# Low parts of the weights by an accumulating transfer onto a negated copy, in a two-layer hybrid trunk kernel

## The chip, the cores and the metric

One core of one Trainium2 chip runs the whole program. The metric is the device time of one execution in microseconds (us). Engines are named as in the profile: PE (TensorE matmul), PEld (its weight load), DVE (VectorE), ACT (ScalarE), POOL (GpSimd), SP (SyncE); ACTq, SPq and POOLq are their instruction queues.

## The reference, cut to what matters

A two-layer decoder trunk of width 1024 runs over 1024 prompt tokens and 32 sample tokens. Per layer: RMSNorm, one input projection to 3592 columns, four token mixers side by side (S5, HGRN2, mLSTM, retention), a gate, one output projection, the residual.

```python
for l in range(DEPTH):                                  # DEPTH = 2
    h = rmsnorm(x, norm_w[l])
    proj = jnp.einsum('bld,de->ble', h, w_in[l])        # (., 1024) x (1024, 3592)
    ...                                                 # four mixers on slices of proj, head norms, gates
    x = x + jnp.einsum('ble,ed->bld', mixed, w_out[l])  # (., 1024) x (1024, 1024)
y = rmsnorm(x, final_norm_w)
```

## The kernel before, in words

**Passes and blocks.** Each layer is done in two passes of 512 prompt tokens; the second pass of a layer (passes 1 and 3) carries the 32 sample tokens too. In a pass the input projection runs over 14 blocks of 256 columns (one, `ml_ifg`, has 264), each block with all 1024 rows of the weights as 8 tiles of 128 rows (`KT` = 8). That makes 56 input blocks (4 x 14). In the text they are numbered from 0 in the order in which they run. The output projection has blocks of its own (`"wo"`), which are used without being split.

**High and low parts.** An input block is multiplied as three products, x high by w high, x high by w low and x low by w high, of tensors of type float32r. `split_high` (ACT, lines 1225 to 1233) rounds the raw weights `wraw` to `whi` in one instruction over 2048 (or 2112) columns. `split_low` (POOL, lines 1179 to 1190) then writes `wlo = wraw - whi` in eight instructions, one for each row tile. `wraw`, `whi` and `wlo` each have two slots. The sample tokens of blocks with tokens on the output's rows (`tiled`, line 2376) are multiplied with `wraw` in plain float32, ahead of the block's other pieces.

**Order.** `make_plan` writes one order of steps, which all engines follow; `PLACES` puts the projection's pieces between the steps of the mixers, so that PE has projection work while DVE and ACT work on a mixer. The split of a block is a step at the first piece of the block before it (`split_after`). There ACT splits, and then asks for the weights of the block after the next (`load_until`, line 1250), which go into the slot of the block that has just begun; for that it waits until this block is split. A split waits for the last piece of the block two back (same slot) and for its own weights.

**What PE waits for.** In the first piece of a block PE waits for each row tile's low part before the three products of that tile (lines 2371, 2372); the order of products is tile by tile. A piece is 24 matmuls: 8 row tiles by three products.

**What else POOL does.** In the plan's order, on the same queue as `split_low`: the powers for the RMSNorm of the token tiles (`power`, lines 1192 to 1200) and for the head norms (lines 1211 and 1214), for which DVE waits.

Of the kernel before, what the change touches and what calls it, by code (L numbers as in the profile page):

```python
# [18 lines left out]
F32 = mybir.dt.float32  # L19
# [6 lines left out]
P = 128  # L26
# [372 lines left out]
def trunk_kernel(nc, inp, out, parts=("hg", "ml", "rt", "s5")):  # L399
    plan = make_plan(parts)  # L400
    ctx = ExitStack()
    with ctx:
# [119 lines left out]
        wraw = sb("wraw", [P, 2, KT, WC])  # L522
        with nc.sbuf_tensor("tail_w", [P, 2, KT, WC], F32) as tail_w:
            pass
        whi = sb("whi", [P, 2, KT, WC], F32R)
        wlo = sb("wlo", [P, 2, KT, WC], F32R)
# [171 lines left out]
        def tail_weights(b):  # L698
            if b < 2:
                return wraw[:, wslot[(LAST, "wo", b)], :, 0:256]  # L700
            return tail_w[:, hslot[(LAST, ("s5_x", "s5_g")[b - 2])], :, 0:256]
# [28 lines left out]
        wlo_done = signal("wlo_done", [b + (g,) for b in in_blocks for g in range(KT)])  # L730
# [160 lines left out]
        def _(sp):  # L891
# [52 lines left out]
            for k in w_loads[:2]:  # L944
                src, width = weight_columns(k)
                sp.dma_start(wraw[:, wslot[k], :, 0:width], src.rearrange("(k p) c -> p k c", p=P)).then_inc(*wr_in[wslot[k]].inc(k))
# [224 lines left out]
        def _(pool):  # L1171
# [49 lines left out]
        def _(act):  # L1221
# [15 lines left out]
            def load_until(i):  # L1237
                while loads and len(w_loads) - len(loads) <= i:
# [11 lines left out]
                    nc.scalar.dma_start(wraw[:, wslot[k], :, 0:width], src.rearrange("(k p) c -> p k c", p=P)).then_inc(*wr_in[wslot[k]].inc(k))  # L1250
# [1086 lines left out]
        def _(pe):  # L2337
# [6 lines left out]
            for s, part in plan:  # L2344
# [12 lines left out]
                elif s[0] == "proj" and part[0] in ("mm", "mm2"):  # L2357
# [3 lines left out]
                    for k in [part[1]]:  # L2361
# [8 lines left out]
                        for kt in range(*((0, 4) if part[0] == "mm" else (4, KT)) if long_piece(k) else (KT,)):  # L2370
                            if k == pieces_of_block(*b)[0]:
                                pe.wait_ge(*wlo_done.at(b + (kt,)))
                            if tiled(k):
                                width = BLOCK[b[1]][2] // 4
                                for g in range(4):
                                    mm = nc.tensor.matmul(bank.t[TS * g:TS * g + TS, 0:width], mixT[:, kt, HALF:W], wraw[:, wslot[b], kt, g * width:(g + 1) * width],
                                                          start=kt == 0, stop=kt == KT - 1)
                                continue
                            for x, w in ((hhi, whi), (hhi, wlo), (hlo, whi)):
                                first, last = kt == 0 and w is whi and x is hhi, kt == KT - 1 and x is hlo  # L2380
                                if BLOCK[b[1]][3] == "ch":
                                    _, c0, ln = piece_psum(k)
                                    c = slice(c0, c0 + ln)
                                    mm = nc.tensor.matmul(bank.t[:, 0:c.stop - c.start], w[:, sl, kt, k[2] * P:(k[2] + 1) * P], x[:, kt, c],  # L2384
                                                          start=first, stop=last)
                                else:
                                    c = slice(k[2] * P, k[2] * P + P)
                                    width = BLOCK[b[1]][2]
                                    mm = nc.tensor.matmul(bank.t[:, 0:width], x[:, kt, c], w[:, sl, kt, 0:width], start=first, stop=last)  # L2389
                        if kt == KT - 1:  # L2390
# [307 lines left out]
                elif s[0] == "out":  # L2698
# [13 lines left out]
                    for kt, row in enumerate(mix_order(n)):  # L2712
                        if r == TS:
                            for g in range(4):
                                mm = nc.tensor.matmul(bank.t[TS * g:TS * g + TS, 0:64], mixT[:, row, k[2] * P:k[2] * P + r], wraw[:, wslot[b], kt, 64 * g:64 * g + 64],
                                                      start=kt == 0, stop=kt == 7)
                            continue
                        mm = nc.tensor.matmul(bank.t[0:r, 0:256], mixT[:, row, k[2] * P:k[2] * P + r], wraw[:, wslot[b], kt, 0:256],  # L2718
# [28 lines left out]
```

## Time and profile before

| What | Value |
|---|---|
| median of 3 runs | 1543.24 us (1541.05 to 1543.25) |
| profiled execution | 1546.32 us, of which the span from its first to its last instruction is 1544.5 us |
| PE busy | 1376.2 us (89% of the span) |
| PEld busy | 1205.4 us (78%) |
| DVE busy | 889.5 us (58%) |
| ACT busy | 549.8 us (36%) |
| POOL busy | 445.5 us (29%) |
| granted TensorE clock, mean | 0.934 |
| DMA | 149.84 MB, 97 GB/s |

An engine's busy share is an average over stages with different limits. A busy PE is not PE at its peak, as matmuls overlap. The chain of work that ended last is followed back from the last instruction, at each step to what released it, or to the instruction before it on its engine; what stands on this chain set the end of this execution.

### The profile page before, as it was taken

How to read it: one execution, taken by the hardware profiler on the slowest of the kernel's cores; microseconds unless marked ns; L12 is line 12 of the kernel's file. 1: busy time of each engine (PE TensorE's matmuls, PEld its weight loads, DVE VectorE, ACT ScalarE, POOL GpSimd, SP SyncE). 2: the span in 40 equal slices, each digit the busy share in tenths (PEclk: the TensorE clock that was granted, in tenths of full speed). 3: DMA queues.
4: the chain of work that ended last, by engine and by line, in shares of the span. 5: the costliest groups of instructions: out<-in, count | busy, mean ns of one | idle time of the engine just before them, and what ended most of it. 6: DMA issues, size and time to landing. Idle time of an engine off the chain costs nothing.

```text
span 1544.5 us, 31690 instructions
## 1 busy us (share of the span) xinstructions
PE 1376.2 (89%) x12391; PEld 1205.4 (78%) x12391; DVE 889.5 (58%) x2670; ACT 549.8 (36%) x1197; POOL 445.5 (29%) x628
## 2 busy tenths in 40 slices
PE   2868899989898999998999899998999999889896
PEld 2757789778786889876787789987878898779665
DVE  4986746463697535555746543656456444644537
ACT  4435443324333533322452334332642533421011
POOL 4341533522002351432310154352200433331001
PEclk9988999989898999998999999997999999999889
DMA  6322123422233423342322333342313415354501
GB/s 176 96 82 71 55 85 110 130 73 87 59 101 120 130 70 108 102 106 70 113 67 86 113 102 112 109 144 59 114 59 118 111 58 125 137 112 95 148 10 59
DMA packets 167563, 149.84 MB, mean 97 GB/s; under 512 B 63440, under 2 KB 155352, under 8 KB 165752
## 3 DMA queue, kind: packets, MB, share of 16 engines
q1 hardware_dynamic: 96696, 76.38, 17.7%
q10 hardware_dynamic: 70720, 71.44, 15.2%
q8 instruction: 100, 1.64, 0.5%
q14 instruction: 47, 0.39, 0.1%
HBM read 124.42 MB, written 23.37 MB: 96 GB/s over the span
## 4 chain that ended last, share of the span: by engine, by line
PE 64%; DVE 19%; ACT 6%; issue 5%; POOL 3%; DMA 1%; SPq 1%; DVEq 0%; ACTq 0%; POOLq 0%
PE psum L2389 17%; PE psum L2384 16%; PE psum L2718 6%; DVE r L1723 4%; PE psum L2696 3%; PE psum L2637 3%; DVE r L2097 3%; PE psum L2548 2%; PE psum L2636 2%; PE psum L2456 2%; POOL rs L1214 1%; ACT r L1504 1%; POOL wlo L1189 1%; PE psum L2634 1%; DVE QE L2118 1%
## 5 line engine op out<-in xcount | busy, mean ns | idle before, releaser
L1189 POOL TENSOR_TENSOR wlo<-wraw,whi 128x256 fp32r<-128x256 f32 (+1 forms) x448 | 345.9, 807 | 425.9 <-ACT whi L1233 425.9
L2389 PE MATMUL psum<-whi,hhi 128*128 128x256 f32 (+1 forms) x896 | 267.7, 299 | 4.3 <-ACT th L1320 2.0
L2389 PE MATMUL psum<-whi,hlo 128*128 128x256 f32 (+1 forms) x896 | 259.0, 289 | 0.0
L2389 PE MATMUL psum<-wlo,hhi 128*128 128x256 f32 (+1 forms) x896 | 258.6, 289 | 0.0
L2384 PE MATMUL psum<-hhi,whi 128*128 128x288 f32 (+2 forms) x672 | 231.7, 345 | 7.8 <-ACT r L1354 5.6
L2384 PE MATMUL psum<-hhi,wlo 128*128 128x288 f32 (+2 forms) x672 | 220.3, 328 | 0.0
L2384 PE MATMUL psum<-hlo,whi 128*128 128x288 f32 (+2 forms) x672 | 220.3, 328 | 0.0
L2718 PE MATMUL psum<-wraw,mixT 128*128 128x256 f32 x768 | 179.8, 395 | 6.8 <-DVE xo L2314 6.8
L2389 PEld LDWEIGHTS psum<-whi,hhi 128*128 128x128 f32 x896 | 176.9, 197 | 11.1 <-issue 7.0
L2389 PEld LDWEIGHTS psum<-wlo,hhi 128*128 128x128 f32 x896 | 177.0, 198 | 0.7 <-issue 0.5
L1211 POOL TENSOR_SCALAR rs<-mv 128x4 f32<-128x4 f32 (+1 forms) x54 | 10.4, 192 | 575.1 <-DVE mv L2280 574.3
L2389 PEld LDWEIGHTS psum<-whi,hlo 128*128 128x128 f32 x896 | 176.1, 196 | 0.0
L2718 PEld LDWEIGHTS psum<-wraw,mixT 128*128 128x128 f32 x768 | 150.2, 198 | 29.8 <-DVE xo L2314 7.8
L2384 PEld LDWEIGHTS psum<-hhi,whi 128*128 128x128 f32 x672 | 129.7, 193 | 23.3 <-issue 12.4
L1233 ACT ACTIVATE whi<-wraw 128x2048 fp32r<-128x2048 f32 (+1 forms) x56 | 107.3, 1916 | 113.1 <-PE psum L2384 54.2
L2384 PEld LDWEIGHTS psum<-hhi,wlo 128*128 128x128 f32 x672 | 129.7, 193 | 12.4 <-issue 3.4
L2384 PEld LDWEIGHTS psum<-hlo,whi 128*128 128x128 f32 x672 | 129.2, 192 | 10.3
L2277 DVE BATCH_NORM_STATS2 stats<-psum 128x6 f32<-128x64 f32 (+1 forms) x144 | 22.3, 217 | 99.0 <-PE psum L2637 98.9
L2637 PE MATMUL psum<-r,ST 128*128 128x64 f32 (+1 forms) x384 | 70.0, 286 | 2.2 <-issue 2.2
L2097 DVE TENSOR_TENSOR r<-r 128x256 f32<-128x256 f32 (+1 forms) x134 | 53.0, 467 | 15.5 <-PE psum L2548 15.4
L2637 PEld LDWEIGHTS psum<-r,ST 128*128 128x128 f32 x384 | 58.4, 203 | 4.0 <-issue 3.7
L1214 POOL TENSOR_TENSOR rs<-rs,epow 128x4 f32<-128x4 f32 (+1 forms) x54 | 56.7, 1050 | 4.5
(355 smaller groups left out, 2298.6 us busy)
## 6 DMA issues: line engine op xcount, KB each, us to landing
wraw<-in_w_in ACTq DMA_DIRECT2D x50, 1024.0 KB, 5.4
wraw<-in_w_out ACTq DMA_DIRECT2D x14, 1024.0 KB, 5.5
x<-xo SPq DMA_DIRECT2D x48, 128.0 KB, 2.3
r<-x SPq DMA_DIRECT2D x10, 512.0 KB, 5.4
r<-in_c_rot SPq DMA_DIRECT2D x4, 1088.0 KB, 7.2
wraw<-in_w_in ACTq DMA_DIRECT2D x4, 1056.0 KB, 5.9
r<-WTm SPq DMA_DIRECT2D x4, 1024.0 KB, 11.9
r<-VTm SPq DMA_DIRECT2D x4, 1024.0 KB, 5.9
```

The lines of the kernel that those rows point to most:

```text
L1189: nc.gpsimd.tensor_tensor(wlo[:, hslot[b], ks, 0:width], wraw[:, wslot[b], ks, 0:width], whi[:, hslot[b], ks, 0:width].bitcast(F32), ALU.s ...
L1214: nc.gpsimd.tensor_tensor(rs[0:T, :], rs[0:T, :], epow[0:T, :], ALU.pow).then_inc(*rs_done.inc(s))
L1233: nc.scalar.activation(whi[:, hslot[b], :, 0:width], wraw[:, wslot[b], :, 0:width], ACT.Copy).then_inc(*whi_done.inc(b))
L1723: nc.vector.tensor_tensor(o, a, b, op).then_inc(*dve_done.inc())
L2097: nc.vector.tensor_tensor(e, x, x[:, :, at - 1:at].broadcast_to([P, 2 * T // blk, blk]), ALU.subtract).then_inc(*(dve_done.inc() if w else ...
L2384: mm = nc.tensor.matmul(bank.t[:, 0:c.stop - c.start], w[:, sl, kt, k[2] * P:(k[2] + 1) * P], x[:, kt, c], start=first, stop=last)
L2389: mm = nc.tensor.matmul(bank.t[:, 0:width], x[:, kt, c], w[:, sl, kt, 0:width], start=first, stop=last)
L2456: yield nc.tensor.matmul(out(q, a), X(h, ri, q), V_rows(s[1], h, ri, q)[:, v], start=False, stop=ri == 1)
L2548: return nc.tensor.matmul(o.rearrange("p (a x) -> p a x", a=2), E[:, i, k0:k0 + kn], QE[:, i, :, q0:q0 + qn], start=True, stop=True)
L2637: mm = nc.tensor.matmul(o, stt[0:T, h, 0:T], v(h), start=br == "ml", stop=True)
L2696: mm = nc.tensor.matmul(bank.t[r * g:r * g + r, 0:w], x, wo[:, kt, g * w:(g + 1) * w], start=kt == kts[0], stop=kt == kts[-1])
L2718: mm = nc.tensor.matmul(bank.t[0:r, 0:256], mixT[:, row, k[2] * P:k[2] * P + r], wraw[:, wslot[b], kt, 0:256], start=kt == 0, stop=kt == 7)
```

## The change

`whi` is still one rounding copy of `wraw` by ACT. The low part is now made in two steps: ACT first writes `wlo = -round(wraw)` (a second copy, with scale -1), and then a DMA issued by POOL adds `wraw` onto `wlo` in place. One transfer has at most 2048 elements of a partition, so a block of 256 columns takes one transfer of 1 MB and the blocks of 264 columns two halves (`parts_of`). The three buffers lie densely for a block (`weights`), so that a transfer's row is contiguous. The negated copy goes ahead of the high one on ACT. In the first piece that uses the low parts, PE does all high products first and then the low ones, each behind a wait for the transfer; a `tiled` piece waits for no low part. The next load of `wraw` waits for the transfers instead of POOL's subtractions.

```diff
@@ split_low, on POOL
-                prev = before(in_blocks, b, 2)
-                if prev is not None:
-                    pool.wait_ge(*PB[bank_of[last_piece[prev]]].full.at(last_piece[prev]))
-                pool.wait_ge(*whi_done.at(b))
-                width = BLOCK[b[1]][2]
-                for g in range(KT):
-                    ks = slice(g, g + 1)
-                    nc.gpsimd.tensor_tensor(wlo[:, hslot[b], ks, 0:width], wraw[:, wslot[b], ks, 0:width],
-                                            whi[:, hslot[b], ks, 0:width].bitcast(F32), ALU.subtract).then_inc(*wlo_done.inc(b + (g,)))
+                for h in range(parts_of(b)):
+                    c = weight_part(b, h)
+                    pool.wait_ge(*wneg_done.at(b + (h,)))
+                    nc.gpsimd.dma_start(wlo[:, hslot[b], c].bitcast(F32), wraw[:, wslot[b], c], accum_op=ALU.add).then_inc(*wlo_sum[hslot[b], h].inc(b))
@@ split_high, on ACT
-                width = BLOCK[b[1]][2]
-                nc.scalar.activation(whi[:, hslot[b], :, 0:width], wraw[:, wslot[b], :, 0:width], ACT.Copy).then_inc(*whi_done.inc(b))
+                for h in range(parts_of(b)):
+                    c = weight_part(b, h)
+                    nc.scalar.activation(wlo[:, hslot[b], c], wraw[:, wslot[b], c], ACT.Copy, scale=-1.0).then_inc(*wneg_done.inc(b + (h,)))
+                c = slice(0, KT * BLOCK[b[1]][2])
+                nc.scalar.activation(whi[:, hslot[b], c], wraw[:, wslot[b], c], ACT.Copy).then_inc(*whi_done.inc(b))
@@ load_until, on ACT
-                        act.wait_ge(*wlo_done.at(prev + (KT - 1,)))
+                        for kt in (KT // 2 - 1, KT - 1):
+                            act.wait_ge(*wlo_ready(prev, kt))
@@ the products, on PE
-                        for kt in range(*((0, 4) if part[0] == "mm" else (4, KT)) if long_piece(k) else (KT,)):
-                            if k == pieces_of_block(*b)[0]:
-                                pe.wait_ge(*wlo_done.at(b + (kt,)))
...
+                            new = k == [q for q in pieces_of_block(*b) if not tiled(q)][0]
+                            three = ((hhi, whi), (hhi, wlo), (hlo, whi))
+                            order = [(kt, x, w) for kt in kts for x, w in three]
+                            if new:
+                                order = [o for o in order if o[2] is whi] + [o for o in order if o[2] is wlo]
+                            for kt, x, w in order:
+                                if new and w is wlo:
+                                    pe.wait_ge(*wlo_ready(b, kt))
```

The new helpers:

```python
def parts_of(b):
    return 1 if BLOCK[b[1]][2] == 256 else 2

wlo_sum = {(a, h): signal(f"wlo_sum{a}{h}", [b for b in in_blocks if hslot[b] == a and h < parts_of(b)], 16) for a in range(2) for h in range(2)}

def wlo_ready(b, kt):
    return wlo_sum[hslot[b], kt * parts_of(b) // KT].at(b)

def weight_part(b, h):
    size = KT * BLOCK[b[1]][2] // parts_of(b)
    return slice(h * size, (h + 1) * size)
```

## Rows read from the trace of the kernel before

**Rows 1.** The page: busy time by engine, and the chain that ended last by engine.

```profile
PE 1376.2 (89%) x12391; PEld 1205.4 (78%) x12391; DVE 889.5 (58%) x2670; ACT 549.8 (36%) x1197; POOL 445.5 (29%) x628
...
PE 64%; DVE 19%; ACT 6%; issue 5%; POOL 3%; DMA 1%; SPq 1%; DVEq 0%; ACTq 0%; POOLq 0%
```

**Rows 2.** The page, costliest groups: busy us, mean ns, idle before and its releaser.

```profile
L1189 POOL TENSOR_TENSOR wlo<-wraw,whi 128x256 fp32r<-128x256 f32 (+1 forms) x448 | 345.9, 807 | 425.9 <-ACT whi L1233 425.9
...
L1233 ACT ACTIVATE whi<-wraw 128x2048 fp32r<-128x2048 f32 (+1 forms) x56 | 107.3, 1916 | 113.1 <-PE psum L2384 54.2
```

**Rows 3.** The chain in order of time: start, length in us, what.

```profile
24.07 6.51 POOL wlo L1189 x8
...
285.02 5.61 POOL wlo L1189 x8
...
1204.43 5.88 POOL wlo L1189 x8
```

**Rows 4.** DVE groups by form in 36 to 101 us (S5 set-up, layer 0).

```profile
L1723 DVE TENSOR_TENSOR r<-s5p,r 128x576 f32<-128x576 f32 x8 | 9.2, 1192 | 0.1
...
L1723 DVE TENSOR_TENSOR r<-r 128x8 f32<-128x8 f32 x6 | 2.6, 464 | 0.1
```

**Rows 5.** The same in 400 to 476 us (S5 set-up, layer 1).

```profile
L1723 DVE TENSOR_TENSOR r<-s5p,r 128x576 f32<-128x576 f32 x8 | 5.7, 754 | 0.2
...
L1723 DVE TENSOR_TENSOR r<-r 128x8 f32<-128x8 f32 x6 | 0.9, 172 | 0.1
```

**Rows 6.** Busy us of the engines in one stretch, clock, DMA share, GB/s.

```profile
36.00:101.00 65.00, 50.31 (x292) 43.97 (x292) 61.37 (x148) 24.83 (x37) 30.60 (x32) 0.92 0.30 90
```

**Rows 7.** The chain again: HGRN's products on DVE.

```profile
132.31 4.61 DVE r L2110 x7
...
156.09 4.63 DVE r L2110 x7
...
167.36 6.58 DVE r L2097 x8
...
402.31 2.69 DVE r L2097 x8
...
479.43 5.71 DVE r L2097 x7
```

**Rows 8.** Timeline of DVE near 178 us.

```profile
178.31 1.50 DVE L2110 TENSOR_TENSOR r<-r 128x128 f32<-128x128 f32 x7
```

**Rows 9.** The chain where it passes ACT's rounding copy.

```profile
128.57 1.91 ACT whi L1233
...
152.42 1.79 issue
...
1228.11 1.92 ACT whi L1233
```

**Rows 10.** Timeline: rounding copies of blocks 3 and 46, and PE's first matmuls of each.

```profile
72.54 1.90 ACT L1233 ACTIVATE whi<-wraw 128x2048 fp32r<-128x2048 f32 x1
...
80.40 0.28 PE L2389 MATMUL psum<-whi,hhi 128*128 128x256 f32 x1
...
1202.33 1.96 ACT L1233 ACTIVATE whi<-wraw 128x2112 fp32r<-128x2112 f32 x1
...
1206.93 0.74 PE L2376 MATMUL psum<-wraw,mixT 128*32 128x66 f32 x32
```

**Rows 11.** Timeline: the same two of block 20.

```profile
524.36 1.92 ACT L1233 ACTIVATE whi<-wraw 128x2048 fp32r<-128x2048 f32 x1
...
539.58 0.28 PE L2384 MATMUL psum<-hhi,whi 128*128 128x256 f32 x1
```

**Rows 12.** DMA issues with KB each and us to landing; the last row is of `r<-WTm`, 1024 KB.

```profile
wraw<-in_w_in ACTq DMA_DIRECT2D x50, 1024.0 KB, 5.4
...
x<-xo SPq DMA_DIRECT2D x48, 128.0 KB, 2.3
...
DMA to landing us min/median/max: 6.7/11.9/16.4
```

More of the change, by code:

```diff
@@ L521, in trunk_kernel, with weights @@
         hlo = sb("hlo", [P, KT, W], F32R)
-        wraw = sb("wraw", [P, 2, KT, WC])
-        with nc.sbuf_tensor("tail_w", [P, 2, KT, WC], F32) as tail_w:
-            pass
-        whi = sb("whi", [P, 2, KT, WC], F32R)
-        wlo = sb("wlo", [P, 2, KT, WC], F32R)
+        wraw = sb("wraw", [P, 2, KT * WC])
+        with nc.sbuf_tensor("tail_w", [P, 2, KT * WC], F32) as tail_w:
+            pass
+        whi = sb("whi", [P, 2, KT * WC], F32R)
+        wlo = sb("wlo", [P, 2, KT * WC], F32R)
+        def weights(buf, slot, width=256):
+            return buf[:, slot, 0:KT * width].rearrange("p (k c) -> p k c", k=KT)
         mixT = sb("mixT", [P, 10, W])
@@ L699, in tail_weights @@
             if b < 2:
-                return wraw[:, wslot[(LAST, "wo", b)], :, 0:256]
-            return tail_w[:, hslot[(LAST, ("s5_x", "s5_g")[b - 2])], :, 0:256]
+                return weights(wraw, wslot[(LAST, "wo", b)])
+            return weights(tail_w, hslot[(LAST, ("s5_x", "s5_g")[b - 2])])
         def x_rows(x, n, t):
@@ L729, in trunk_kernel @@
         whi_done = signal("whi_done", in_blocks)
-        wlo_done = signal("wlo_done", [b + (g,) for b in in_blocks for g in range(KT)])
+        def parts_of(b):
+            return 1 if BLOCK[b[1]][2] == 256 else 2
+        wneg_done = signal("wneg_done", [b + (h,) for b in in_blocks for h in range(parts_of(b))])
+        wlo_sum = {(a, h): signal(f"wlo_sum{a}{h}", [b for b in in_blocks if hslot[b] == a and h < parts_of(b)], 16) for a in range(2) for h in range(2)}
[4 more added lines that the diff above has]
+            return slice(h * size, (h + 1) * size)
         th_keys = [k for k in pieces if BLOCK[k[1]][4] == "av"]
@@ L945, in _ @@
                 src, width = weight_columns(k)
-                sp.dma_start(wraw[:, wslot[k], :, 0:width], src.rearrange("(k p) c -> p k c", p=P)).then_inc(*wr_in[wslot[k]].inc(k))
+                sp.dma_start(weights(wraw, wslot[k], width), src.rearrange("(k p) c -> p k c", p=P)).then_inc(*wr_in[wslot[k]].inc(k))
             def permuted(ap, t):
@@ L2369, in _ @@
                                     pe.wait_ge(*PB[bank_of[u]].free.at(u))
-                        for kt in range(*((0, 4) if part[0] == "mm" else (4, KT)) if long_piece(k) else (KT,)):
-                            if k == pieces_of_block(*b)[0]:
-                                pe.wait_ge(*wlo_done.at(b + (kt,)))
-                            if tiled(k):
-                                width = BLOCK[b[1]][2] // 4
+                        kts = range(*((0, 4) if part[0] == "mm" else (4, KT)) if long_piece(k) else (KT,))
@@ L2375, in _ @@
+                        width = BLOCK[b[1]][2]
+                        if tiled(k):
+                            width //= 4
+                            for kt in kts:
                                 for g in range(4):
-                                    mm = nc.tensor.matmul(bank.t[TS * g:TS * g + TS, 0:width], mixT[:, kt, HALF:W], wraw[:, wslot[b], kt, g * width:(g + 1) * width],
+                                    mm = nc.tensor.matmul(bank.t[TS * g:TS * g + TS, 0:width], mixT[:, kt, HALF:W], weights(wraw, wslot[b], 4 * width)[:, kt, g * width:(g + 1) * width],
@@ L2377, in _ @@
                                                           start=kt == 0, stop=kt == KT - 1)
-                                continue
-                            for x, w in ((hhi, whi), (hhi, wlo), (hlo, whi)):
-                                first, last = kt == 0 and w is whi and x is hhi, kt == KT - 1 and x is hlo
+                        else:
+                            new = k == [q for q in pieces_of_block(*b) if not tiled(q)][0]
[6 more added lines that the diff above has]
+                                    pe.wait_ge(*wlo_ready(b, kt))
+                                first, last = kt == 0 and w is whi and x is hhi, (kt, x, w) == order[-1] and kt == KT - 1
+                                wv = weights(w, sl, width)
@@ L2390, in _ @@
-                        if kt == KT - 1:
+                                    mm = nc.tensor.matmul(bank.t[:, 0:ln], wv[:, kt, k[2] * P:(k[2] + 1) * P], x[:, kt, c0:c0 + ln], start=first, stop=last)
+                                else:
+                                    mm = nc.tensor.matmul(bank.t[:, 0:width], x[:, kt, k[2] * P:k[2] * P + P], wv[:, kt, :], start=first, stop=last)
+                        if kts[-1] == KT - 1:
                             mm.then_inc(*bank.full.inc(k))
@@ L2714, in _ @@
                             for g in range(4):
-                                mm = nc.tensor.matmul(bank.t[TS * g:TS * g + TS, 0:64], mixT[:, row, k[2] * P:k[2] * P + r], wraw[:, wslot[b], kt, 64 * g:64 * g + 64],
+                                mm = nc.tensor.matmul(bank.t[TS * g:TS * g + TS, 0:64], mixT[:, row, k[2] * P:k[2] * P + r], weights(wraw, wslot[b])[:, kt, 64 * g:64 * g + 64],
                                                       start=kt == 0, stop=kt == 7)
                             continue
-                        mm = nc.tensor.matmul(bank.t[0:r, 0:256], mixT[:, row, k[2] * P:k[2] * P + r], wraw[:, wslot[b], kt, 0:256],
+                        mm = nc.tensor.matmul(bank.t[0:r, 0:256], mixT[:, row, k[2] * P:k[2] * P + r], weights(wraw, wslot[b])[:, kt, :],
                                               start=kt == 0, stop=kt == 7)
```

8 lines of the change are left out of this document (1 added, 7 removed).

## The prediction

> **What bounds the kernel now.** I read the page first. PE is busy 89% of the span, DVE 58%, POOL 29%, and the chain that ended last lies 64% on PE, 19% on DVE, 6% on ACT and only 3% on POOL [rows 1]. So most of the span is matmul work that this change neither adds nor removes. What can be won is the part of the chain that is not PE.
>
> The groups tell what the change touches: 448 subtractions on POOL, 345.9 us busy, and 56 rounding copies on ACT of 1.92 us each [rows 2]. POOL's 346 us are three quarters of its 445.5 us, yet they stand on the chain in three places only: 6.51 us at 24 us, 5.61 us at 285 us, 5.88 us at 1204 us [rows 3]. Read as a queue, POOL is not the bound.
>
> It costs in a second way that no wait shows. I compared DVE's durations of the same instruction with and without POOL's subtractions beside it. The S5 set-up of layer 0 runs at 36 to 101 us with 30.6 us of POOL work in the window [rows 6], that of layer 1 at 400 to 476 us without any subtraction. The 576-column products take 1192 ns in the first and 754 ns in the second, the 8-column ones 464 and 172 ns [rows 4, 5]. In HGRN, seven products of line 2110 take 4.61 and 4.63 us on the chain beside POOL, and 1.50 us alone [rows 7, 8]; those of line 2097 take 6.58 us for eight beside POOL, 2.69 us alone, and 5.71 us for seven beside it [rows 7]. DVE operations with two inputs in SBUF wait for POOL's. The reader is to see that these stretched operations lie on the chain.
>
> **Part 1: POOL's subtractions go.** The stretch of DVE that I can read from rows: 8 x (1192 - 754) = 3.5 us and 6 x (464 - 172) = 1.8 us in the set-up, 5.3 us together; the other forms of that window are stretched too, and I leave them as an upside. DVE is busy 61.4 of those 65 us and PE 50.3 [rows 6], so DVE is the bound there and I take the 5.3 us whole. In HGRN: (4.61 - 1.50) + (4.63 - 1.50) + (6.58 - 2.69) + (5.71 - 7/8 x 2.69) = 3.11 + 3.13 + 3.89 + 3.36 = 13.5 us. Between these pieces the chain runs over PE, whose projection pieces fill the time beside DVE, so that a shorter DVE step soon meets a busy PE. The bounds are nothing and 13.5; I take three quarters, 10 us.
>
> The three places on the chain: at 24 us and at 285 us the RMSNorm powers stand behind eight subtractions on POOL's queue. In their stead stands one DMA issue, but ACT's square sums, which the powers need, come 1.9 us later behind the additional copy. What issuing a transfer costs POOL stands in no row; the bounds are nothing and the 2.3 us in which a whole 128 KB transfer is issued and lands [rows 12], and I take 1 us. So 6.5 - 1.9 - 1 = 3.6 us and 5.6 - 1.9 - 1 = 2.7 us, 6.3 us together. At 1204 us PE waited for the subtractions row tile by row tile in a `tiled` piece, which now waits for no low part: it began at 1206.93 [rows 10] and its last row tile waited until 1204.43 + 5.88 = 1210.31 [rows 3], while 64 such matmuls need some 1.1 us (32 records took 0.74). That gives 1210.8 - 1206.9 - 1.1 = 2.8 us. Together 9.1 us.
>
> **Part 2: the negated copy on ACT.** 56 more copies of 1.92 us, 107 us of ACT, which goes from 550 to 657 us. PE's projection pieces and ACT's idle time hide it in most places. On the chain a copy stands at 128 us and 1228 us, and at 152 us the "issue" of 1.79 us is the time of the copy as well [rows 9]. In each of these, operations that a mixer needs are queued behind the copy on ACT. 3 x 1.9 = 5.7 us. If the cover were gone everywhere it would be 107 us; nothing on the chain speaks for more than a few further places. At least it costs nothing.
>
> **Part 3: how late the low parts are.** Before, they were complete 8 x 0.77 = 6.2 us after `whi` (345.9 us by 448) [rows 2]. Now the transfer is issued when the negated copy ends, 1.9 us after the start of the split, and lands T later. PE can do the high products first: 16 of a piece's 24 matmuls, 1.9 us. So T may be as long as (PE's first matmul + 1.9 us, + 1.1 us if a `tiled` piece goes first) - (start of split + 1.9 us). Block 46: 1206.93 + 3.0 - 1204.24 = 5.7 us. Block 3: 80.40 + 1.9 - 74.45 = 7.9 us [rows 10]. Block 20: 539.58 + 1.9 - 526.26 = 15.2 us [rows 11]. The same reading for all 56 blocks gives 8.9, 9.7 and 10.0 us for the next three and at least 11.6 us for the others, half of them within 15.5. A block that stalls PE gives its successor as much more time, so that stalls in a row don't add. With that, the stalls sum to 0.3 us for T = 6, 2.4 for 8, 7.8 for 10, 18 for 12, 46 for 15 and 128 for 20.
>
> T isn't shown. A load of 1 MB lands in 5.4 us, a transfer of 128 KB in 2.3 us [rows 12]: about 1.9 us fixed and 3.5 us for each MB. An accumulation has two streams of 1 MB to read, so 1.9 + 7.0 = 8.9 us. The next load of `wraw` is asked for beside it at most blocks, and may add up to 3.5 us; the slowest 1 MB transfer of the trace took 16.4 us [rows 12]. The bounds are 5.4 and 16.4 us; I take 10 us, as it is nearest to the load's row: 7.8 us of stalls.
>
> The Trainium skill ("Collectives: The Full Stack", Part 3, on the bandwidth ceiling) says that an add in the DMA path costs no cycles of its own but needs two source reads, and so runs at half the rate of a copy; its fit in "DMA: Bandwidth & Descriptors" (Anatomy of one DMA) of 2.0 us plus the bytes at 436 GB/s would make an estimate of 6.8 us for two megabytes, and the stalls about 1 us instead of 7.8. No run here shows either yet.
>
> **Part 4: the rest.** The bytes of the DMA engines grow by at least 56 MB, over a mean busy share that is 0.30 in the window shown [rows 6]; DMA is 1% of the chain [rows 1]. I count nothing, and 0 to 5 us in the range. The number of matmuls, their forms and PE's waits stay. The output blocks don't change.
>
> **Sum.** 5.3 + 10 + 9.1 = 24.4 us won, 5.7 + 7.8 = 13.5 us lost: 10.9 us. The profiled execution has 1546.3 us with 1.8 us outside its span, 3.1 us above the median; the difference is put onto the median: 1543.2 - 10.9 = 1532 us.
>
> **The rivals.** *The transfers land late.* If the add has a rate limit of its own, or the loads beside it take the engines, T is 15 us or more. For it: nothing in the trace bounds an accumulation, and the slowest 1 MB transfer took three times the usual one. Against it: the bytes. At T = 15 the sum is 24.4 - 5.7 - 46 = -27, 1570 us; at 20, 1652 us. The gains are used up where the stalls reach 18.7 us, at T = 12.1 us. This one ends slower, and it is the step that decides.
>
> *Descriptors wait for DVE.* A transfer of POOL's needs POOL to write its descriptors, and DVE has just been seen to share a path with POOL. DVE is idle only 3.6 of 65 us in the set-up [rows 6]; if the issue has to fit between DVE's operations, each up to 1.2 us, T grows by one or two of these, to 12: 18 us of stalls, 1542 us, no change. The Trainium skill ("SBUF — State Buffer", Who interferes with whom) states this against the change: a DVE operation in a two-port mode locks POOL out of writing descriptors until it ends, whereas a product of two SBUF tensors is inferred there not to.
>
> *The relief is hidden.* PE is busy 89%; if DVE's shorter steps only make it wait for PE, of 5.3 + 10 = 15.3 us a third remains: 1532 + 10 = 1542 us, no change.
>
> *All of it arrives.* With T at 8 us and the stretch of all forms gone, 5.3 + 5 (for the forms left out) + 13.5 + 9.1 - 5.7 - 2.4 = 24.8 us: 1518 us.
>
> **How the numbers follow.** The forecast (T from 8 to 12, relief mostly real) 0.46; all of it 0.13; late transfers 0.24; descriptors wait 0.08; relief hidden 0.09. The measurement can tell about 0.2%, 3 us, from no change. Faster: 0.46 + 0.13 = 0.59, and 0.02 from the edges of the hidden cases: 0.61. Same: 0.12, the rest of these two on the near side. Slower: 0.24 + 0.03 = 0.27. The range goes down to 1510 (all of it, with T at 6 and no copy on the chain) and up to 1570 (T = 15); beyond it are the long transfers, some 0.13, and little below. The likeliest case's own range is 1520 to 1541.
>
> **What would show it.** Right: line 2097 and 2110 at 0.42 and 0.29 us in every place; no subtraction on POOL's queue; powers at 24 and 285 us some 3.5 us earlier; transfers landing within 8 to 12 us; PE idle before its first low product in about five blocks. Wrong: landings of 15 us or more, with PE's waits for `wlo_sum` at the head of the list of waits; or ACT's share of the chain well above 6% with waits of DVE and PE for ACT behind the negated copies; or DVE durations unchanged.

## The result

| kernel | median | runs | ratio to the kernel before, 95% interval |
|---|---|---|---|
| before | 1543.24 us | 1541.05 to 1549.28 | |
| changed | 1523.1 us | 1517.42 to 1525.83 | 0.9859 [0.9819, 0.9898] |

Each row has four runs. The change saves 20 us, 1.4% (1.0 to 1.8%). The profiled execution of the changed kernel took 1525.83 us, 1524.0 of them its span. I had put it at 1532 us, within 1510 to 1570: the sign and the range hold, but the gain is nearly twice the forecast, and the experiments will show that it is what is left of a relief and of costs that I had both made far too small.

**The profile after.** The page: busy time by engine and the chain that ended last, as in [rows 1].

```profile
PE 1365.6 (90%) x12391; PEld 1199.0 (79%) x12391; DVE 816.8 (54%) x2670; ACT 650.0 (43%) x1257; POOL 153.4 (10%) x240
...
PE 66%; DVE 13%; ACT 8%; DMA 5%; issue 5%; SPq 2%; POOL 1%; ACTq 0%; DVEq 0%; POOLq 0%
```

DVE executes the same 2670 instructions in 72.7 us less. ACT has the 100 us of the second copy. On the chain DVE falls from 19 to 13%, POOL from 3 to 1%, and ACT rises from 6 to 8%; DMA, which was 1%, is now 5%, with another 2% for SP's queue. That last pair of numbers is what I had not expected. PE, with the same 12391 matmuls, is busy for 10.6 us less, at a mean granted clock of 0.941 instead of 0.934; no run separates this share of the gain from the rest.

The groups that stand where [rows 2] stood (busy us, mean ns, idle before and its releaser), and one of PE's with its wait for the transfers:

```profile
L2411 PE MATMUL psum<-wlo,hhi 128*128 128x256 f32 (+1 forms) x896 | 227.2, 290 | 7.9 <-DMA wlo<-wraw 7.9
...
L1248 ACT ACTIVATE wlo<-wraw 128x2048 fp32r<-128x2048 f32 (+1 forms) x60 | 107.6, 1800 | 118.3 <-PE psum L2409 54.1
L1204 POOL DMA_DIRECT2D wlo<-wraw x60 | 54.1, 914 | 550.7 <-ACT wlo L1248 550.3
L1250 ACT ACTIVATE whi<-wraw 128x2048 fp32r<-128x2048 f32 (+1 forms) x56 | 106.5, 1903 | 0.0
```

The DMA issues, with KB and us to landing [rows 12]:

```profile
wlo<-wraw POOLq DMA_DIRECT2D x52, 1024.0 KB, 9.0
wraw<-in_w_in ACTq DMA_DIRECT2D x50, 1024.0 KB, 5.9
x<-xo SPq DMA_DIRECT2D x48, 128.0 KB, 2.4
r<-x SPq DMA_DIRECT2D x10, 512.0 KB, 9.2
```

A transfer of 1 MB lands in 9.0 us; from the load's row I had worked out 8.9 and taken 10. But look at the last line: ten loads of 512 KB, which the change doesn't touch, now take 9.2 us at the median, where the page of before has 5.4.

DVE's durations in the S5 set-up of layer 0, 36 to 101 us, are now those that [rows 5] had for layer 1 without POOL:

```profile
L1741 DVE TENSOR_TENSOR r<-s5p,r 128x576 f32<-128x576 f32 x8 | 5.7, 754 | 0.1
...
L1741 DVE TENSOR_TENSOR r<-r 128x8 f32<-128x8 f32 x6 | 0.9, 172 | 0.1
```

And HGRN's seven products on the timeline, beside DVE's other work, take 1.50 us where [rows 7] had 4.61 to 4.63:

```profile
115.09 1.50 DVE L2128 TENSOR_TENSOR r<-r 128x128 f32<-128x128 f32 x7
```

**Where the gain arises.** I cut both traces at the same matmuls, so that each pair of windows holds the same work. Columns are those of [rows 6]: the stretch, its length, busy PE, PEld, DVE, ACT, POOL, clock, DMA share, GB/s. The kernel before, from the set-up to block 4 and from block 4 to block 8:

```profile
36.00:120.50 84.50, 63.43 (x471) 54.87 (x471) 71.12 (x180) 35.82 (x53) 30.60 (x32) 0.86 0.28 85
120.50:199.30 78.80, 67.52 (x661) 60.18 (x662) 53.35 (x156) 36.95 (x71) 28.82 (x38) 0.91 0.21 59
```

The changed kernel, the same work:

```profile
33.00:102.30 69.30, 59.82 (x471) 52.75 (x471) 56.18 (x180) 43.07 (x59) 4.39 (x5) 0.93 0.69 174
102.30:172.10 69.80, 64.16 (x660) 57.29 (x661) 40.96 (x156) 43.86 (x75) 7.26 (x10) 0.95 0.55 129
```

The same 180 instructions of DVE take 56.2 us instead of 71.1, and the stage is 15.2 us shorter; in the next stage DVE saves 12.4 us and the stage 9.0. PE sits idle for 9.5 us of the first stage instead of 21.1, and its granted clock is higher (0.86 to 0.93, then 0.91 to 0.95). The DMA share beside it goes from 0.28 to 0.69.

**Where it goes again.** How far each kernel is ahead of the one before at the first matmul of some blocks (from the traces, us), with kernels that are explained below:

| block, time in before | no low parts | negated copy only | changed | three blocks spared |
|---|---|---|---|---|
| 3, 80 us | 12.8 | 7.2 | 7.1 | 7.3 |
| 4, 120 us | 21.6 | 18.3 | 18.2 | 18.2 |
| 9, 222 us | 34.9 | 28.5 | 28.5 | 28.7 |
| 18, 504 us | 45.3 | 38.6 | 38.9 | 38.4 |
| 27, 692 us | 51.7 | 42.0 | 39.1 | 41.9 |
| 28, 736 us | 50.0 | 40.1 | 33.0 | 39.9 |
| 46, 1207 us | 56.9 | 43.8 | 36.4 | 40.0 |
| 48, 1244 us | 57.0 | 38.9 | 27.3 | 35.3 |
| 54, 1381 us | 60.3 | 40.2 | 22.0 | 33.4 |
| end of the span | 58.4 | 42.3 | 20.5 | 35.5 |

The changed kernel is 39 us ahead at block 27 and ends 20.5 us ahead. These are single profiled executions, so that a difference of 2 or 3 us between two columns means little. A final figure of -20 us hides a gain of 39 and a loss of 19 behind it.

### The profile page after: what moved, and what is told of

It reads as the page before. It is cut to its first block, busy times and chain, and to the rows that moved or that the text cites. A ratio compares the mean times of both kernels' runs of the same rounds, so it can differ in the third digit from the quotient of the medians.

```text
span 1524.0 us, 31308 instructions
## 1 busy us (share of the span) xinstructions
PE 1365.6 (90%) x12391; PEld 1199.0 (79%) x12391; DVE 816.8 (54%) x2670; ACT 650.0 (43%) x1257; POOL 153.4 (10%) x240
## 3 DMA queue, kind: packets, MB, share of 16 engines
q1 hardware_dynamic: 96696, 76.38, 18.2%
## 4 chain that ended last, share of the span: by engine, by line
PE 66%; DVE 13%; ACT 8%; DMA 5%; issue 5%; SPq 2%; POOL 1%; ACTq 0%; DVEq 0%; POOLq 0%
PE psum L2409 18%; PE psum L2411 17%; PE psum L2740 5%; PE psum L2718 3%; PE psum L2659 3%; DVE r L2115 2%; PE psum L2570 2%; DVE r L1741 2%; PE psum L2478 2%; PE psum L2658 2%; DMA wraw<-in_w_in 1%; ACT r L1522 1%; PE psum L2656 1%; ACT whi L1250 1%; PE psum L2473 1%
## 5 line engine op out<-in xcount | busy, mean ns | idle before, releaser
L2411 PE MATMUL psum<-whi,hhi 128*128 128x256 f32 (+1 forms) x896 | 258.5, 297 | 12.2 <-ACT th L1338 5.2
L2411 PE MATMUL psum<-whi,hlo 128*128 128x256 f32 (+1 forms) x896 | 250.8, 289 | 0.0
L2411 PE MATMUL psum<-wlo,hhi 128*128 128x256 f32 (+1 forms) x896 | 227.2, 290 | 7.9 <-DMA wlo<-wraw 7.9
L2409 PE MATMUL psum<-hlo,whi 128*128 128x288 f32 (+2 forms) x672 | 216.5, 328 | 0.0
L2411 PEld LDWEIGHTS psum<-whi,hhi 128*128 128x128 f32 x896 | 176.3, 197 | 15.2 <-issue 13.0
L2409 PE MATMUL psum<-hhi,wlo 128*128 128x288 f32 (+2 forms) x672 | 188.1, 324 | 0.0
L2740 PE MATMUL psum<-wraw,mixT 128*128 128x256 f32 x768 | 175.4, 388 | 3.3 <-DVE xo L2332 3.3
L2411 PEld LDWEIGHTS psum<-wlo,hhi 128*128 128x128 f32 x896 | 161.3, 196 | 9.0 <-DMA wlo<-wraw 8.5
L1248 ACT ACTIVATE wlo<-wraw 128x2048 fp32r<-128x2048 f32 (+1 forms) x60 | 107.6, 1800 | 118.3 <-PE psum L2409 54.1
L2409 PEld LDWEIGHTS psum<-hhi,wlo 128*128 128x128 f32 x672 | 120.3, 189 | 10.9 <-issue 1.4
L1204 POOL DMA_DIRECT2D wlo<-wraw x60 | 54.1, 914 | 550.7 <-ACT wlo L1248 550.3
```

The costliest lines, as they stand in the source:

```text
L1204: nc.gpsimd.dma_start(wlo[:, hslot[b], c].bitcast(F32), wraw[:, wslot[b], c], accum_op=ALU.add).then_inc(*wlo_sum[hslot[b], h].inc(b))
L1248: nc.scalar.activation(wlo[:, hslot[b], c], wraw[:, wslot[b], c], ACT.Copy, scale=-1.0).then_inc(*wneg_done.inc(b + (h,)))
L2409: mm = nc.tensor.matmul(bank.t[:, 0:ln], wv[:, kt, k[2] * P:(k[2] + 1) * P], x[:, kt, c0:c0 + ln], start=first, stop=last)
L2411: mm = nc.tensor.matmul(bank.t[:, 0:width], x[:, kt, k[2] * P:k[2] * P + P], wv[:, kt, :], start=first, stop=last)
```

## The experiments

**Taking the change apart.** Three kernels climb from nothing to the whole change. In the first, no low part is made at all, and PE multiplies with the high part in its place, so that what it computes is less exact.

```diff
@@ split_low and split_high
-                    pool.wait_ge(*wneg_done.at(b + (h,)))
-                    nc.gpsimd.dma_start(wlo[:, hslot[b], c].bitcast(F32), wraw[:, wslot[b], c], accum_op=ALU.add)...
-                    nc.scalar.activation(wlo[:, hslot[b], c], wraw[:, wslot[b], c], ACT.Copy, scale=-1.0)...
@@ the products
-                                wv = weights(w, sl, width)
+                                wv = weights(whi, sl, width)
```

> Leaves the low parts out altogether: no subtraction, no negated copy, no transfer; PE multiplies with the high part in the low part's place (the output is then less exact), in the new order of products. It holds every gain of the change and none of its costs. If POOL's subtractions stretched DVE (my theory), it gains more than the change: 1543 less some 30 to 45 us, about 1505. If the change's gain came from the order of products alone, it gives no more than the change did, about 1523.

Measured: 1489.54 us (1488.14 to 1489.94), 0.9647 [0.963, 0.9664]. In this order of products, all that POOL's subtractions cost is 54 us, more than the 30 to 45 that I had expected. DVE is busy 816.4 us.

The second adds ACT's negated copy back; the transfer stays out, and PE waits for the copy and multiplies with it as it is.

```diff
@@ against the changed kernel, split_low
-                    nc.gpsimd.dma_start(wlo[:, hslot[b], c].bitcast(F32), wraw[:, wslot[b], c], accum_op=ALU.add)...
```

> The change without its transfer: ACT writes the negated copy and PE multiplies with it as it is. Against e1 it adds ACT's 56 copies alone. My prediction has three places on the chain, 5.7 us: about 6 us above e1. The rival, that ACT's copies are passed by the chain in many places, wants 20 us or more above e1.

Measured: 1504.56 us (1504.26 to 1508.05), 0.9751 [0.9732, 0.977]. The copies cost 15 us, between the two values expected (6 and 20). In the table above the two kernels are 5.6 us apart at block 3, 3.3 at block 4, 6.4 at block 9, 9.7 at block 27 and 16.1 at the end: most of it is lost a few us at a time.

The third makes all copies and all transfers, but PE never waits for them: it takes the high part where the low one stood. (ACT's next split waits for the transfers two blocks back, so that the slot is free. This adds no idle time: before its negated copies ACT stands idle for loads or issues 43.5 us in six places, as against 43.1 us in six in the changed kernel.)

```diff
@@ against the changed kernel, the products
-                                if new and w is wlo:
-                                    pe.wait_ge(*wlo_ready(b, kt))
...
-                                wv = weights(w, sl, width)
+                                wv = weights(whi, sl, width)
```

> The change with all its copies and transfers, but PE multiplies with the high part in the low part's place and doesn't wait for a transfer; the next negated copy into the slot and the next load do. Against e2 it adds the traffic and what it slows, against the change it lacks the lateness. If lateness is the transfers' cost (my table gives 2.4 to 7.8 us for landings of 8 to 10 us), it is 3 to 8 us below the change, and level with e2. If contention with other transfers is the cost, it is level with the change and well above e2.

Measured: 1525.4 us (1521.34 to 1526.29), 0.9877 [0.9859, 0.9894]. It isn't faster than the changed kernel (1523.1). So the lateness of the low parts costs nothing that can be measured here, and 21 us are the price of the transfers' mere presence: 1525.4 - 1504.6. I had counted that as nothing.

**The order of the products alone.** The kernel before, with PE's new order and with `tiled` pieces that wait for no low part.

```diff
@@ the products, in the kernel before
+                            if new:
+                                order = [o for o in order if o[2] is whi] + [o for o in order if o[2] is wlo]
```

> The kernel before with PE's part of the change alone: high products first, low ones behind the waits, no wait for low parts in the tiled pieces; the low parts are still POOL's subtractions. My prediction gives this 2.8 us (the piece at 1204 us) and little besides: 1538 to 1543. The rival, that the order of products is what helped, wants half of the gain or more, 1533 or less.

Measured: 1543.9 us (twelve runs, 1536.33 to 1552.03), 0.9993 [0.9972, 1.0015]. The order by itself isn't what helped. The 2.8 us forecast for it don't show, though the interval, some 3 us to either side, doesn't exclude them.

**Why POOL's subtractions cost 54 us.** There are two candidates: DVE's operations wait for POOL's accesses to SBUF, or POOL's queue holds up the powers behind the subtractions. Both kernels put eight dummy instructions of 256 columns behind each block's transfer, one after the other; they differ only in what POOL does. The first reads two constants and subtracts, the second only writes.

```diff
@@ split_low, behind the transfer
+                for g in range(KT):
+                    if g >= 0:
+                        pool.wait_ge(*pool_done.now())
+                    nc.gpsimd.tensor_tensor(spare[:, 0], const[:, 0:256], const[:, 256:512], ALU.subtract).then_inc(*pool_done.inc())
@@ and, in the second kernel, in its place
+                    nc.gpsimd.memset(spare[:, 0], 0.0).then_inc(*pool_done.inc())
```

> The change, with eight subtractions of two 256-column tiles of constants put on POOL behind every block's transfer; their result is not used. They read SBUF twice as the old ones did and hold POOL's queue as long. If DVE's relief and POOL's free queue are the gain, the time goes back to that of before or above it, since the costs of the change stay: 1543 to 1560, with DVE busy some 70 us more than in the change. If not, it stays near 1523.

> The same with eight memsets of 256 columns in place of the eight subtractions: POOL's queue is held, but POOL reads nothing. If DVE waits only for POOL's reads, DVE's busy time stays near 817 us and the time within about 5 us of the change. If any work of POOL stretches DVE, DVE's busy time rises as in e5, in proportion to POOL's busy time.

Measured: 1620.05 us (1615.16 to 1627.1) with subtractions, 1.0498 [1.0475, 1.0521]; 1525.86 us (1522.82 to 1531.3) with memsets, 0.9878 [0.9862, 0.9895]. Busy time in the first:

```profile
PE 1402.9 (87%) x12391; PEld 1226.4 (76%) x12391; DVE 915.0 (57%) x2670; ACT 649.8 (40%) x1257; POOL 512.8 (32%) x688
...
L1211 POOL TENSOR_TENSOR spare_t<-const 128x256 f32<-128x256 f32 x448 | 373.9, 835 | 30.7
```

and in the second:

```profile
PE 1371.0 (90%) x12391; PEld 1203.2 (79%) x12391; DVE 816.9 (53%) x2670; ACT 649.7 (42%) x1257; POOL 294.8 (19%) x688
...
L1211 POOL MEMSET spare_t<- 128x256 f32 x448 | 159.6, 356 | 22.5
```

With 448 subtractions beside it DVE takes 98 us more than in the changed kernel for the same work; with 448 memsets DVE's time doesn't move (816.9 against 816.8), nor does the kernel's by more than 3 us, though POOL's queue is held for another 182 us (159.6 busy and 22.5 idle before it). So it is POOL's reading, not its being busy, that stretches DVE. The Trainium skill ("SBUF — State Buffer", Who interferes with whom) says the same: a DVE operation with two SBUF inputs contends with a GpSimd operation that reads SBUF, and not with one that only writes. DVE's busy time in these two runs agrees.

The queue's part is not separated by them, as a subtraction holds POOL for 835 ns and a memset for 356. The chains by engine, with subtractions and with memsets:

```profile
PE 53%; DVE 19%; ACT 7%; issue 7%; DMA 6%; POOL 5%; SPq 2%; ACTq 0%; DVEq 0%; POOLq 0%
```

```profile
PE 66%; DVE 13%; ACT 7%; DMA 5%; issue 5%; SPq 2%; POOL 1%; ACTq 0%; DVEq 0%; POOLq 0%
```

DVE's share grows by 6 points of the span and POOL's by 4. The dummy subtractions alone stand on the chain with 2.3% of the span, 37 us, and DVE's waits for the head norms' powers behind them grow from 40.6 to 66.9 us. So most of the 94 us between the two kernels is on DVE, but not all, and the same goes for the 54 us: on the chain of the kernel before, POOL's own subtractions stand with 18 us [rows 3]. I had expected 1543 to 1560 us with the dummy subtractions and missed it by 60. They cost 97 us over the changed kernel where the real ones had cost 54; DVE is stretched by 98 us instead of 73, and the rest of the difference stays open.

**ACT's order.** The high copy first, the negated one second: PE's first products and the mixers get `whi` 1.9 us sooner, the transfer goes 1.9 us later.

```diff
@@ split_high
+                nc.scalar.activation(whi[:, hslot[b], c], wraw[:, wslot[b], c], ACT.Copy).then_inc(*whi_done.inc(b))
                 for h in range(parts_of(b)):
...
-                nc.scalar.activation(whi[:, hslot[b], c], wraw[:, wslot[b], c], ACT.Copy).then_inc(*whi_done.inc(b))
```

> The change with ACT's two copies swapped: the high parts are ready 1.9 us earlier, the transfers are issued 1.9 us later. If lateness of transfers counts, the time goes up as if landings took 1.9 us longer, by some 5 us (from T = 9 to 11 in the table of stalls); if the late high parts count more, it goes down by a few us.

Measured: 1528.06 us (1525.81 to 1534.56), 0.9908 [0.9889, 0.9926]. Worse by 5 us at the median, as expected if lateness counts; the ranges of the two kernels just touch (1525.83 and 1525.81 us), so the size is uncertain. 1.9 us more of lateness on every transfer seems to cost something, and the slack that the third kernel showed is thin. PE's own weight loads (PEld) wait for transfers six times instead of three (12.5 us against 8.5).

**The transfer's size.** Two transfers of 512 KB for each block.

```diff
@@ parts_of
-            return 1 if BLOCK[b[1]][2] == 256 else 2
+            return 2
```

> The change with every block's copy and transfer in two halves, so that the first half is issued 1 us earlier and PE can begin with the low products of four row tiles, at the price of 52 more copies (a few tenths of a us each) and 52 more issues of 0.9 us on POOL. If the landing of the whole MB is what PE waits for, it gains up to 3 us; if a transfer's fixed time and POOL's issues count, it loses 3 us or more.

Measured: 1520.88 us (1519.83 to 1525.92), 0.9859 [0.9842, 0.9876]: the same as the changed kernel. Half the bytes land in 8.2 us at the median, almost the 9.0 us of the whole; as two of them are in flight together there, this doesn't tell what one alone would take. POOL makes 112 issues of 0.88 us where it made 60 of 0.91, 44 us more.

**Which transfers carry the 21 us?** Three falls of the table hold most of the loss: from block 27 to 28, from 46 to 48, and between 48 and 54 (in the traces, from block 53 to 54). There the changed kernel loses 4.2, 4.2 and 6.6 us more than the one with the copy only, 15.0 of the 21.8 us by which the two differ at the end. On the chain of the changed kernel each has a DMA that isn't a transfer of this change. First, in pass 1, the store of `ud` (S5's input, which goes out to a DRAM tensor and comes back in another layout) and the string of SP's loads behind it (start, length, what):

```profile
656.75 11.23 DMA ud<-r
668.37 0.45 SPq L1029
...
677.94 2.47 DMA sst<-in_state_ret
680.45 1.92 PE psum L2656 x16
```

POOL had issued the transfer of block 28 at 654.88. In the kernel with the copy only, SP issues this store and goes on 4.0 us later, not 11.2:

```profile
653.81 0.37 SPq L1020 DMA_DIRECT2D ud<-r  x1
657.78 7.08 SPq L1029 DMA_DIRECT2D r<-ud  x12
```

Second, a load of weights, issued 1 us behind the first of the two transfers of block 46 (`ml_ifg`), on which ACT, then PE wait:

```profile
1165.90 2.06 ACT wlo L1248 x2
1168.49 13.17 DMA wraw<-in_w_in
```

and the same step in the kernel with the copy only:

```profile
1161.17 7.22 DMA wraw<-in_w_in
```

Third, SP's small state loads, beside the transfer of block 54, which POOL issued at 1327.54:

```profile
1327.58 2.19 SPq L1132
1329.82 1.16 SPq L1132
1331.02 3.76 SPq L1132
1334.82 4.37 DMA sst<-in_state_mlstm_n
1339.24 1.07 PE psum L2659 x8
```

Here even the issues become slow, up to 3.76 us each; what slows an issue, no run isolates. All eight take 12.4 us, against 8.0 us in the kernel with the copy only. In each of the three places an engine waits for the landing, so that there is no slack, and all are loads and stores that the change leaves alone. The DMA engines are busier there than on the mean: 0.74 of 645 to 680 us, 0.85 of 1165 to 1182 and 0.84 of 1320 to 1340, against 0.53 of the whole span.

A test by removal: in these three blocks alone POOL subtracts as before, and in a control the same edit is made on three other blocks.

```diff
+        by_pool = [in_blocks[i] for i in (28, 46, 54)]      # the control: (23, 44, 51)
...
@@ split_low
+                if b in by_pool:
+                    width = BLOCK[b[1]][2]
+                    pool.wait_ge(*whi_done.at(b))
+                    for g in range(KT):
+                        nc.gpsimd.tensor_tensor(weights(wlo, hslot[b], width)[:, g, :], weights(wraw, wslot[b], width)[:, g, :],
+                                                weights(whi, hslot[b], width)[:, g, :].bitcast(F32), ALU.subtract).then_inc(*wlo_done.inc(b + (g,)))
+                    return
@@ split_high
-                for h in range(parts_of(b)):
+                for h in range(0 if b in by_pool else parts_of(b)):
```

> The changed kernel, but in blocks 28, 46 and 54 the low part is made by POOL's eight subtractions as before, with no negated copy and no transfer; the other 53 blocks are as changed, and all products are computed. In the changed kernel's trace a DMA stands on the chain beside the transfer of each of these three: a store of ud that takes 11.2 us at 656.8 us (4.0 us in the kernel without transfers), a load of wraw that takes 13.2 us at 1168.5 us (6.9 us there), and SP's issue of eight small state loads that takes 12.3 us at 1323.3 us (8.0 us there). Theory A: the 21 us that the transfers' traffic costs are carried by these three meetings. Then this kernel gains 7.2 + 6.3 + 4.3 = 17.8 us less up to 3 us for POOL's subtractions beside DVE: 1505 to 1509 us. Theory B: the cost is spread over all transfers, or the next meeting takes the place of the one removed. Then three of 56 blocks are worth 1 to 2 us, 1521 to 1523 us.

> The same edit on three other blocks, 23, 44 and 51, beside whose transfers no DMA stands on the chain; all products are computed. Theory A: no gain, 1522 to 1526 us. Theory B: the same 1 to 2 us as in the kernel with blocks 28, 46 and 54 spared, so that the two agree within 3 us.

Measured: 1506.59 us (1505.57 to 1510.8) with blocks 28, 46 and 54 spared, 0.9764 [0.9743, 0.9786]; 1526.61 us (1523.38 to 1527.48) in the control, 0.9885 [0.9864, 0.9906]. Three of 56 blocks give 17 us against the changed kernel and 20 against the control; three others give nothing. Theory A holds. The edit takes out the negated copy of these blocks as well, but the control loses its copies too, and the kernel with the copy only, which has all three, doesn't lose this time. In the traces the gain over the changed kernel stands at the three places: 4.2, 4.5 and 6.3 us, 15.0 in sum. The kernel with three blocks spared still makes 56 transfers (55.68 MB) and stands 2 us above the one that makes none, with intervals that overlap; so all the other transfers together cost at most a few us. Its chain at the weights' load, and its timeline of SP's queue at the third place:

```profile
1164.88 7.08 DMA wraw<-in_w_in
```

```profile
1316.83 4.16 SPq L1136 DMA_DIRECT2D sst<-in_state_mlstm_C  x4
1321.03 4.50 SPq L1136 DMA_DIRECT2D sst<-in_state_mlstm_n  x4
```

The load takes 7.1 us instead of 13.2, and SP issues the eight state loads in 8.7 us instead of the 12.4 of the changed kernel:

```profile
1323.28 4.25 SPq L1132 DMA_DIRECT2D sst<-in_state_mlstm_C  x4
1327.58 8.06 SPq L1132 DMA_DIRECT2D sst<-in_state_mlstm_n  x4
```

(The first four are as slow with block 54 spared as without; the gain is in the last four.) SP issues the `ud` store of pass 1 at 652.13 and goes on at 659.40: 7.3 us instead of 11.2, and the store is no longer on the chain. The store of pass 0, at 270.5 us, stands there instead, with 9.4 us, and costs little: around it this kernel falls back by about 1 us against the changed one. A store that takes longer is no loss by itself: in the kernel before, the one of pass 1 took 7.0 us and was not on the chain. The kernel with three blocks spared is also the fastest complete one of this study, 37 us ahead of the one before and 17 ahead of the changed one.

**DVE instead of both.** No transfer, no negated copy; DVE subtracts, one step of the plan after ACT's high copy.

```diff
@@ DVE's loop over the plan
+            def low_parts():
+                b = low_blocks.pop(0)
+                width, n = BLOCK[b[1]][2], KT // LOW_PARTS      # LOW_PARTS = 2
+                dve.wait_ge(*whi_done.at(b))
+                for h in range(LOW_PARTS):
+                    v = [weights(t, sl, width)[:, h * n:(h + 1) * n, :] for t, sl in ((wlo, hslot[b]), (wraw, wslot[b]), (whi, hslot[b]))]
+                    nc.vector.tensor_tensor(v[0], v[1], v[2].bitcast(F32), ALU.subtract).then_inc(*wlo_done.inc(b + (h,)))
```

> No transfer and no negated copy, and POOL subtracts nothing: DVE makes each block's low part with two subtractions of 1024 columns, one step of the plan after ACT's high copy; PE's order of products is the changed kernel's, and all products are computed. A product of 256 columns takes DVE 0.34 us with POOL idle, so a block costs about 2.5 us and 56 blocks 140 us: DVE busy 816 + 140 = 956 us. Theory A (what hurt was POOL and DVE in SBUF together, and the DMA traffic; an engine's own work is hidden as ACT's is): ACT's 107 us of copies cost 15 us, so DVE's 140 us cost 20 to 30 us over the 1489.5 us of the kernel without low parts: 1510 to 1520 us, faster than the changed kernel. Theory B (DVE, with 13 to 19% of the chain, is the engine that can hide nothing): a third or more of the 140 us shows, 1535 us or more.

Measured: 1527.01 us (1525.56 to 1533.04), 0.9899 [0.9878, 0.9921]: between the two expectations. DVE is busy 943.6 us, so the subtractions take 127 us, of which 37 show: 0.3 of each us, where ACT's copies show 15 of 107, 0.14. DVE has less cover than ACT, as its 21% of this kernel's chain says. Still, 127 us on DVE cost less than POOL's 346 did, 37 against 54 us, and about as much as the changed kernel's copies and transfers together (34 us over the same kernel).

## Why the prediction was right, and where it was not

| term of the sum | forecast | measured | by |
|---|---|---|---|
| relief from POOL's subtractions | 24.4 won | 54 won | before against no low parts |
| negated copies | 5.7 lost | 15 lost | no low parts against copy only |
| lateness | 7.8 lost | nothing measurable | PE not waiting against changed |
| traffic | 0 (0 to 5) lost | 21 lost | copy only against PE not waiting |
| net | 10.9 won | 20 won | |

The time fell into the range in part by luck. The relief was 30 us larger than forecast, and the costs, taken together, 22 us larger; only the difference of these two errors, 7 to 9 us, shows in the result.

**The mechanism of part 1 was right, its size was not.** The products of 576, 128 and 8 columns take 0.75, 0.29 and 0.17 us wherever they stand, and those of line 2097 0.42, as foretold. But I took for the set-up only the two forms whose clean duration I had read in layer 1, 5.3 us, and called the rest an upside. All forms of DVE in that stage lose 14.9 us, and the stage becomes 15.2 us shorter, besides the 3 us by which it begins earlier. The same in the whole kernel: my rows held 18.8 us of stretch (5.3 + 13.5), and DVE's busy time fell by 72.7. The HGRN term was sound: of my 13.5 us, 10.1 lay between blocks 4 and 8, where DVE in all lost 12.4 us and the stage became 9.0 us shorter, copies included, so that little of it was hidden. The rest lies in forms and stages that I had no rows for, and in POOL's queue, as said above. What would have done is in the view itself: compare all forms in two like windows, not two of them. At 24 us the powers came 3.2 us earlier (27.48 against 30.67, forecast 3.6); and the rival of a hidden relief, a third of it left, is refuted by the 54 us. "All of it arrives" (1518 us) came nearer to the time than the forecast, and its relief, 32.9 us, was still too small.

**Part 2 was mis-sized.** I priced three places where a copy stood on the chain of before. The chain shows where a copy stood in the one order that ended last; with DVE's time shortened, ACT came to stand there in more places (6 to 8% of the chain; a share well above 6% was one of my signs of being wrong). That "nothing on the chain speaks for more than a few further places" was the sentence that failed. 15 us is 0.14 of the copies' 107 us.

**Part 3 was right in T and moot in its effect.** T is 9.0 us at the median, from 7.0 to 15.4, by 1.9 us fixed and 3.5 us for each MB of the two streams read. The slowest two, 14.8 and 15.4 us, belong to blocks 26 and 27, whose pieces began only some 10 and 5 us after the landing. PE waits for a transfer in three places, 7.9 us in all, most of it at block 46 (1174.3 to 1180.1 us), where I had 7.8 us over about five. Yet a kernel in which PE waits for none isn't faster. At block 46 one sees why: beside PE, ACT waits for the late load of weights until 1181.7, and PE's next piece waits for ACT. What waits sum to can be more than what they cost.

**Part 4 is the step that failed.** I put the traffic at nothing, and it cost 21 us. I reasoned from the mean DMA share, 0.30, and from DMA's 1% of the chain, and counted nothing. Neither number showed this: what cost was not the mean, but a large transfer meeting a DMA that had no slack. It happened in three of 56 blocks and cost some 17 of 21 us. The order of the plan is fixed, so one might find such meetings in the trace of before: for each transfer's place, which DMA is in flight within 10 us and is waited for. I picked the three from the changed kernel's trace, so that this isn't tried.

**The rivals.** The transfers didn't land late: one of 52 took over 15 us. What this rival had as its reason, large transfers beside loads, was there, but the loads and stores were what paid. Of "descriptors wait for DVE" nothing is seen: POOL issues a transfer in 0.91 us, at least 0.85 and at most 1.21, with DVE busy for 54% of the span. The rule of the Trainium skill that I set beside it ("SBUF — State Buffer", Who interferes with whom) had inferred that a product of two SBUF tensors doesn't lock POOL out, and no run here speaks against that. With the Trainium skill's half rate for an add in the DMA path ("Collectives: The Full Stack", Part 3) the trace agrees roughly: 9.0 us for 1 MB added against 5.9 for 1 MB loaded is 1.5 times, and less the 1.9 us that I had worked out as fixed it is 7.1 against 4.0, 1.8 times. No run has the same transfer without the add. The Trainium skill's fit ("DMA: Bandwidth & Descriptors", Anatomy of one DMA), from which I had made an estimate of 6.8 us, is below all that is measured for 1 MB (7.0 to 15.4).

## What to carry to other kernels

When work is moved to the DMA engines, list the DMAs for which an engine waits without slack and lay the new transfers beside them; three meetings ate some 17 of 39 us here, and sparing those three blocks gave them back. A POOL operation that reads SBUF can be paid for a second time on DVE, as here: compare all of DVE's durations with and without it before calling POOL's time hidden. And when a net result agrees with a sum, take it apart anyway: all four terms of this one were off, and half of what the change could have given lay in the difference.

## What the runs showed of the hardware

- 448 subtractions of 256 columns on POOL, of constants that nobody else uses, lengthen DVE's 2670 instructions from 816.8 to 915.0 us in sum; 448 memsets of the same size leave them at 816.9.
- An accumulating transfer within SBUF takes 9.0 us for 1 MB at the median, and 8.2 us for 512 KB where two halves are issued one behind the other.
- With such transfers in the kernel the 512 KB loads of `r<-x` take 9.2 us instead of 5.4 at the median, and the load of weights on the chain 13.2 us instead of 7.2, where the DMA share is 0.85 (1165 to 1182 us) instead of 0.66 (1158 to 1175 us of the kernel with the copy only).
